# State-space steps of a hybrid encoder block: exponents from running sums read back by row, the z gate from a hyperbolic tangent, and two banks for z

## The reference, cut to what matters

```python
cs = jnp.cumsum((dt * a).reshape(bsz, c, q, g, hg), axis=2)
seg = cs[:, :, :, None] - cs[:, :, None, :]
mask = jnp.tril(jnp.ones((q, q), bool))[None, None, :, :, None, None]
decay = jnp.where(mask, jnp.exp(jnp.where(mask, seg, 0.0)), 0.0)
cb = jnp.einsum('bcqgn,bcsgn->bcqsg', cc, bc)
wts = cb[..., None] * decay
y_diag = jnp.einsum('bcqsgh,bcsghp->bcqghp', wts, xdt)
...
y_off = jnp.einsum('bcqgn,bcghpn->bcqghp', cc, prev) * jnp.exp(cs)[..., None]
```

```python
y = y.reshape(bsz, l, SSD_INNER) * jax.nn.silu(z.astype(F32))
y = y.reshape(bsz, l, SSD_GROUPS, SSD_INNER // SSD_GROUPS)
y = y * lax.rsqrt(jnp.mean(y * y, -1, keepdims=True) + RMS_EPS)
```

## Time and profile before

| | |
|---|---|
| median of 3 runs | 2182.41 us (2177.91 to 2184.29) |
| profiled execution | 2182.37 us, its span 2180.5 us |
| mean granted TensorE clock | 0.952 |
| TensorE busy | 1980.1 us, 91% |
| VectorE busy | 601.0 us, 28% |
| ScalarE busy | 381.4 us, 17% |
| GpSimd busy | 217.7 us, 10% |
| chain that ended last | TensorE 60%, DMA 28%, VectorE 3%, ScalarE 2% |

### The profile page before, as it was taken

How to read it: one execution, slowest core, us unless ns; L and a number is a source line. 1 busy time by engine, 2 the same in 40 slices (tenths; PEclk the granted TensorE clock), 3 DMA queues, 4 the chain that set the end, 5 groups by cost and what they waited for, 6 DMA issues and landing times.

```text
span 2180.5 us, 19987 instructions
## 1 busy us (share of the span) xinstructions
PE 1980.1 (91%) x8382; PEld 938.9 (43%) x8382; DVE 601.0 (28%) x1101; ACT 381.4 (17%) x684; POOL 217.7 (10%) x238
## 2 busy tenths in 40 slices
PE   8989999999989999799988988988988988988887
PEld 4646554456654445434333333334333333333332
DVE  6598756487731115200100100100100100100102
ACT  1334312267740002010000000000000000000001
POOL 1776400022200000000000000000000000000001
PEclk9899999999989999899999999999989999999999
DMA  5622312100104245899999999999999999999995
GB/s 142 126 71 76 112 42 86 58 29 30 58 29 164 69 169 249 356 423 424 428 427 428 428 427 426 428 427 427 428 426 427 428 426 426 429 426 427 428 426 214
DMA packets 88073, 625.47 MB, mean 287 GB/s; under 512 B 21180, under 2 KB 34736, under 8 KB 57776
## 3 DMA queue, kind: packets, MB, share of 16 engines
q1 hardware_dynamic: 75552, 616.41, 68.9%
q10 hardware_dynamic: 12432, 7.79, 1.2%
HBM read 614.39 MB, written 9.78 MB: 286 GB/s over the span
## 4 chain that ended last, share of the span: by engine, by line
PE 60%; DMA 28%; DVE 3%; ACT 2%; issue 1%; POOL 1%; SPq 0%; DVEq 0%; POOLq 0%
PE ps L947 59%; DMA arena<-in_w_e 28%; ACT arena L612 1%; PE ps L1062 0%; DVE arena L1863 0%; DVE arena L1861 0%; DVE arena L1791 0%; DVE arena L1954 0%; DVE arena L1911 0%; ACT L612 0%; POOL arena L492 0%; PE ps L1432 0%; PE ps L1122 0%; DVE arena L1752 0%; DVE arena L1948 0%
## 5 line engine op out<-in xcount | busy, mean ns | idle before, releaser
L947 PE MATMUL ps<-arena 128*64 128x512 f32 (+6 forms) x7850 | 1915.3, 528 | 168.8 <-DMA arena<-in_w_e 107.5
L947 PEld LDWEIGHTS ps<-arena 128*64 128x64 f32 (+2 forms) x7850 | 876.1, 163 | 1183.0 <-issue 1044.5
L612 ACT ACTIVATE arena<-ps 128x512 f32<-128x512 f32 (+5 forms) x292 | 164.8, 595 | 1661.8 <-PE ps L947 954.5
L1920 DVE TENSOR_TENSOR arena<-arena,ps 128x512 f32<-128x512 f32 (+1 forms) x48 | 30.2, 644 | 575.3 <-PE ps L947 575.3
L604 POOL TENSOR_TENSOR arena<-arena 128x1024 f32<-128x1024 f32 x3 | 7.1, 2355 | 1366.2 <-ACT arena L612 1366.2
L1929 DVE TENSOR_TENSOR arena<-arena,ps 128x512 f32<-128x512 f32 x48 | 33.1, 690 | 332.0 <-PE ps L947 332.0
L612 ACT ACTIVATE arena<-arena 128x128 f32<-128x128 f32 (+8 forms) x250 | 110.0, 503 | 82.9 <-DVE arena L1827 20.8
L612 ACT ACT_TABLE_LOAD x74 | 94.9, 1283 | 23.5 <-issue 21.8
L1711 DVE SCALAR_TENSOR_TENSOR arena<-arena 128x512 f32<-128x512 f32 x80 | 60.2, 753 | 2.8
L1911 DVE TENSOR_TENSOR arena<-arena 128x512 f32<-128x512 f32 x8 | 5.6, 694 | 181.9 <-PE ps L1432 181.8
L592 POOL TENSOR_TENSOR arena<-arena 128x768 f32<-128x768 f32 x16 | 24.4, 1524 | 101.2 <-PE ps L947 101.2
(11 more groups left out here) (192 smaller groups left out, 679.8 us busy)
## 6 DMA issues: line engine op xcount, KB each, us to landing
arena<-in_w_e SPq DMA_DIRECT2D x120, 2816.0 KB, 29.3
arena<-in_w_e SPq DMA_DIRECT2D x80, 2048.0 KB, 27.7
arena<-in_w_e SPq DMA_DIRECT2D x16, 1408.0 KB, 22.0
arena<-in_w_in SPq DMA_DIRECT2D x9, 2048.0 KB, 8.4
arena<-in_w_e SPq DMA_DIRECT2D x16, 1024.0 KB, 30.6
arena<-in_w_in SPq DMA_DIRECT2D x5, 1536.0 KB, 6.4
arena<-in_w_out_ssd SPq DMA_DIRECT2D x4, 1536.0 KB, 6.7
gate_scratch<-arena ACTq DMA_DIRECT2D x16, 256.0 KB, 2.4
```

The lines of the kernel that those rows point to most:

```text
L612: return act.activation(out, in_, func, **kw)
L947: return pe.matmul(out, lhsT, rhs, start=a, stop=z)
L1920: tt(o, o, ps[:, i, 0:w], ALU.mult).then_inc(s.hid_ready, 1)
```

## The change

The exponents are no longer products. The running sums of dt·a, which TensorE already forms for another use in bank 5, are copied to `cum` (SBUF, a column per chunk and head), transposed on TensorE, and stored as rows in HBM (`cum_dram`) before the S5 stage. In each step SP loads the rows of six heads and both directions to all 128 partitions (`cum_rows`, two buffers), GpSimd subtracts the token's own sum (`diff_f`, `diff_b`), VectorE takes the smaller of the two directions, and ScalarE takes the exponential in place. Banks 2 and 3 come free: the scores alternate between banks 4 and 2, and z tiles between banks 0 and 3. The four columns of B·C sums of a group are formed at once, and `diag_x` for four chunks at once.

The gate becomes a tanh of z / 2 on ScalarE and a product `(tanh + 1) * z` on VectorE, with the factor 0.5 put into the norm. VectorE's state terms stay in PSUM, and what waited for `y_read` now waits for `gate_ready`.

```diff
+            sp.wait_ge(s.y5_stored, 16 * 2 * T * NQ)
+            sp.wait_ge(s.g_stored, 16 * GATES)
+            sp.wait_ge(s.cum_stored, 16)
+            for i in range(GROUPS * TT):
+                g, c = divmod(i, TT)
+                if i >= 2:
+                    sp.wait_ge(s.diff_ready, i - 1)
+                rows = cum_dram[:, HEADS * c + HG * g:HEADS * c + HG * g + HG, :].rearrange("d h q -> d (h q)")
+                sp.dma_start(cum_rows[:, i % 2].rearrange("p d h q -> p d (h q)"), rows.partition_broadcast(P)).then_inc(cum_loaded[i % 2], 16)
+                if i in (6, 10, 14):
+                    slices(FIRST_Z + 2 + (i - 6) // 4, FIRST_Z + 3 + (i - 6) // 4)
...
+                pool.wait_ge(cum_loaded[i % 2], 16 * (i // 2 + 1))
                 if i >= 1:
-                    pool.wait_ge(s.segm_ps, i)
-                pool.tensor_tensor(rhs_f, first(m_le, HG), last(da[:, c, f], P), ALU.mult)
-                pool.tensor_tensor(rhs_b, first(m_ge, HG), last(da[:, c, b], P), ALU.mult).then_inc(s.mats_ready, 1)
+                    pool.wait_ge(s.diff_min, i)
+                h = slice(HG * g, HG * g + HG)
+                pool.tensor_tensor(diff_f, cum_rows[:, i % 2, 0], last(cum[:, 0, c, h], P), ALU.subtract)
+                pool.tensor_tensor(diff_b, cum_rows[:, i % 2, 1], last(cum[:, 1, c, h], P), ALU.subtract).then_inc(s.diff_ready, 1)
...
-                f(zg[g % 2][:, c, :], ps[:, int(g * TT + c == 1), 0:GI], ACT.Silu).then_inc(s.z_silu, 1)
+                f(zg[g % 2][:, c, :], ps[:, z_bank[c % 2], 0:GI], ACT.Tanh, scale=0.5).then_inc(s.z_tanh, 1)
...
-                act.wait_ge(s.segm_ps, i + 1)
-                if i >= 1:
-                    act.wait_ge(s.g_ready, i)
-                f(emat.rearrange("p (a b) q -> p a (b q)", a=2), ps[:, 2:4, 0:GI], ACT.Exp).then_inc(s.segm_exp, 1)
+                act.wait_ge(s.diff_min, i + 1)
+                f(emat, emat, ACT.Exp).then_inc(s.segm_exp, 1)
...
                 if t >= 2:
-                    pe.wait_ge(s.z_silu, t)
+                    pe.wait_ge(s.z_silu, t - 1)
...
-                pe.wait_ge(s.mats_ready, i + 1)
-                if i >= 1:
-                    pe.wait_ge(s.segm_exp, i)
-                for a in range(2):
-                    o = ps[:, 2 + a, 0:GI].rearrange("p (h q) -> p h q", h=3)
-                    mm(o, m_gt, rhs_f[:, 3 * a:3 * a + 3, :], True, False)
-                    r = mm(o, m_lt, rhs_b[:, 3 * a:3 * a + 3, :], False, True)
-                r.then_inc(s.segm_ps, 1)
...
                 if g + 1 < GROUPS and c < TT - 1:
-                    pe.wait_ge(s.y_read, i + 1)
+                    pe.wait_ge(s.gate_ready, i + 1)
                     added_states(g + 1, c)
...
+            def z_doubled(t):
+
+                g, c = divmod(t, TT)
+                dve.wait_ge(s.z_tanh, t + 1)
+                z = zg[g % 2][:, c]
+                stt(z, z, 1.0, ps[:, z_bank[c % 2], 0:GI], ALU.add, ALU.mult).then_inc(s.z_silu, 1)
+
+            def decay_exponents(i):
+
+                dve.wait_ge(s.diff_ready, i + 1)
+                tt(emat, diff_f, diff_b, ALU.min).then_inc(s.diff_min, 1)
...
+            decay_exponents(0)
             for j in range(TT - 1):
                 weighted_x(0, j)
+                if j == 0:
+                    z_doubled(0)
                 if j == 1:
                     mixing_matrix(0)
+                    decay_exponents(1)
                 carry(0, j)
             mixing_matrix(1)
+            decay_exponents(2)
             for i in range(GROUPS * TT):
...
                 if i >= 1:
                     normalized(i - 1)
+                if i + 1 < GROUPS * TT:
+                    z_doubled(i + 1)
                 if more:
                     weighted_x(g + 1, c)
-                y0, y1, y2 = ty[:, 0], ty[:, 1], ty[:, 2]
-                n.done(tt(h3(y0), h3(xs[:, c, gi]), bc(diag_x[:, i % 2]), ALU.mult))
+                y0, terms = ty[:, 0], []
+                n.done(tt(h3(y0), h3(xs[:, c, gi]), bc(diag_x[:, g % 2, c]), ALU.mult))
                 dve.wait_ge(s.yd_ps, i + 1)
                 if c >= 1:
-                    n.done(tt(h3(y1), h3(ps[:, 6, 0:GI]), bc(e_cs[:, c, f]), ALU.mult))
+                    terms.append(ps[:, 6, 0:GI])
+                    n.done(tt(h3(terms[-1]), h3(terms[-1]), bc(e_cs[:, c, f]), ALU.mult))
...
-                tt(y0, y0, ps[:, 5, 0:GI], ALU.add).then_inc(s.y_read, 1)
-                dve.wait_ge(s.y_read, i + 1)
+                y = ps[:, 5, 0:GI]
+                n.link(tt(y, y, y0, ALU.add))
                 dve.wait_ge(s.z_silu, g * TT + c + 1)
-                tt(ty[:, 3], y0, zg[g % 2][:, c], ALU.mult).then_inc(s.gate_ready, 1)
+                tt(ty[:, 3], y, zg[g % 2][:, c], ALU.mult).then_inc(s.gate_ready, 1)
                 if i + 2 < GROUPS * TT:
                     mixing_matrix(i + 2)
+                if i + 3 < GROUPS * TT:
+                    decay_exponents(i + 3)
                 if more:
                     carry(g + 1, c)
```

More of the change, by code:

```diff
@@ L200, in encoder @@
         dt_bias, a_neg = C.take(2 * HEADS), C.take(2 * HEADS)
-        dt_step, diag_x = C.take(TT, HEADS), C.take(2, HG)
+        dt_step, diag_x = C.take(TT, HEADS), C.take(2, TT, HG)
         d_row, norm_g, ln1_cols = C.take(HEADS), C.take(INNER // P), C.take(2, KT)
@@ L277, in encoder @@
         S = Space(arena, S2.at - 4 * SEQ, top)
-        rhs_f, rhs_b = S.take(HG, P), S.take(HG, P)
+        diff_f, diff_b = S.take(HG, P), S.take(HG, P)
         bc_prod = S.take(SEQ)
+        cum_rows = S.take(2, 2, HG, P)
+        score_bank = (4, 2)
+        z_bank = (0, 3)
         S = Space(arena, late_at, top)
@@ L340, in encoder @@
         slice_loaded = [sem(f"slice_loaded_{i}") for i in range(NW)]
+        cum_loaded = [sem(f"cum_loaded_{i}") for i in range(2)]
         unit_loaded = [sem(f"unit_loaded_{i}") for i in range(LANDINGS)]
@@ L1035, in _ @@
             mm(ps[:, 6, 0:8 * H].rearrange("p (c h) -> p c h", c=TT), ones, da, True, True).then_inc(s.seg_ps, 1)
+            pe.wait_ge(s.seg_exp, 1)
+            for d in range(2):
+                r = pe.transpose(ps[0:TT * H, 3, P * d:P * d + P], cum[:, d].rearrange("p c h -> p (c h)"), ident)
+            r.then_inc(s.seg_ps, 1)
             def toeplitz(q):
@@ L1053, in states @@
                 pe.wait_ge(s.u_loaded, 16 * 2 * T)
+                if q == 0:
+                    pe.wait_ge(s.seg_exp, 2)
                 if q >= 1:
@@ L1141, in added_states, with scores @@
                     mm(ps[:, 6 + d, 0:GI], bn[:, c, P * g:P * g + P], xw[:, d, :], True, True).then_inc(s.st_ps, 1)
-            def scores_and_segments(i):
+            def scores(i):
                 g, c = divmod(i, TT)
-                q = slice(P * c, P * c + P)
-                if i >= 1:
[L1147 to L1150, removed]
-                pe.wait_ge(s.mats_ready, i + 1)
-                if i >= 1:
-                    pe.wait_ge(s.segm_exp, i)
-                for a in range(2):
-                    o = ps[:, 2 + a, 0:GI].rearrange("p (h q) -> p h q", h=3)
-                    mm(o, m_gt, rhs_f[:, 3 * a:3 * a + 3, :], True, False)
-                    r = mm(o, m_lt, rhs_b[:, 3 * a:3 * a + 3, :], False, True)
-                r.then_inc(s.segm_ps, 1)
+                if i >= 2:
+                    pe.wait_ge(s.g_ready, i - 1)
+                if c == 0:
+                    pe.wait_ge(s.bc_ready, g + 1)
+                    for k in range(TT):
+                        mm(ps[:, score_bank[0], P + k:P + k + 1], bc_prod[:, P * k:P * k + P], ones[:, 0:1], True, True)
+                q = slice(P * c, P * c + P)
+                mm(ps[:, score_bank[i % 2], 0:P], bT[:, g, q], cT[:, g, q], True, True).then_inc(s.cb_ps, 1)
             def y_products(i):
@@ L1166, in y_products @@
                 if i >= 1:
-                    pe.wait_ge(s.y_read, i)
+                    pe.wait_ge(s.gate_ready, i)
                 if c >= 1:
@@ L1192, in _ @@
             pe.wait_ge(s.nat_copied, 16)
-            scores_and_segments(0)
+            scores(0)
             pe.wait_ge(s.silu_done, 20)
@@ L1198, in _ @@
                     z_tile(0, j + 1, w)
-            pe.wait_ge(s.z_silu, 2)
-            scores_and_segments(1)
+            scores(1)
             for i in range(GROUPS * TT):
@@ L1204, in _ @@
                 if i + 2 < GROUPS * TT:
-                    scores_and_segments(i + 2)
+                    scores(i + 2)
                 if i >= 1:
@@ L1226, in _ @@
                     pe.wait_ge(s.yt_copied, 3 * GROUPS * TT)
-                    pe.wait_ge(s.y_read, GROUPS * TT)
+                    pe.wait_ge(s.gate_ready, GROUPS * TT)
                 for half in range(halves):
@@ L1742, in carry @@
                         dve.tensor_copy(to, ps[:, 6 + d, 0:GI]).then_inc(s.carried, 1)
-            def mixing_matrix(i):
+            def z_doubled(t):
[6 more added lines that the diff above has]
```

(14 more changed lines are left out.)

34 lines of the change are left out of this document (21 added, 13 removed).

## The result

The changed kernel takes 2200.68 us (median; 2199.17 to 2202.29) against 2182.39 before, a ratio of 1.0087 with a 95% interval of 1.0069 to 1.0105. The forecast was 2199.

What follows compares the result with a forecast made beforehand. The prediction took TensorE to bound the kernel, busy 91% of the span. Loop -2.3, clock +14.4 and start +4.8 us made +16.9 on 2182.4, so 2199 us, with a range of 2181 to 2213.

Steps and rivals of the forecast that it cites:

- TensorE was the bound, and the products taken off it had filled its wait for VectorE: In the steps TensorE sets the pace, busy 47.69 of 48.00 us a group; segment products, 43 us, filled its wait.
- The loop at 47.6 us a group: Between gate products in the steps: 12.8, 12.8, 11.0 and 11.0 us, 47.6 a group; all intervals together -2.3 us.
- The last group at 11.0 a step: In the last group of steps, two steps set by ScalarE at 11.0 us each, the last as it was, 6.0.
- the arm with matrices: ScalarE's work in a step, from the gate product through the root and six matrices to the tanh: 6.4 us.
- The clock, 14.4 us: TensorE's waits in the steps lower its clock: long wait 2.8 us, two short 1.0 each, 14.4 over three groups.
- The start, 4.8 us: Before the first gate product, VectorE's minimum on loaded rows precedes weighted_x: 4.8 us later, bounds 2 and 8.
- Costs at nothing: In the S5 stage, column products, transposes, copies and store cost nothing during TensorE's 6.00 us wait; uncovered, about 1 us.
- rival D: In the steps the row loads are late, each step about 1 us longer: about 2212 us; chance 0.11.
- Rival B: In the steps the clock holds through TensorE's waits and the loop is right: 2182 to 2185 us; chance 0.22.
- Rival C: In the steps VectorE's own work sets the pace, 38.6 us a group, not the loop: 2158 us; chance 0.12.
- The sum: Whole kernel: -2.3 + 14.4 + 4.8 = +16.9 us on 2182.4, giving 2199.

Runs made afterwards that it cites:

- the idle products: Changed kernel with 6 (c = 0) or 3 (c = 1, 2) extra TensorE products before the wait for the gate product; 2184.68 us, ratio 1.0016.
- the rows early: Changed kernel with the first two row loads issued ahead of the two z slices instead of behind them; 2198.29 us, ratio 1.0075.
- the run with the tanh first: Changed kernel with ScalarE's tanh of step i + 2 issued ahead of the six matrices of step i + 3; 2198.78 us, ratio 1.0086.
- the edit with z first: Changed kernel with TensorE's z tile of step i + 2 ahead of the gate product's wait and the added states; 2181.27 us, ratio 1.0002.
- the two reordered engines: Changed kernel with TensorE's z tile ahead of the gate product's wait and ScalarE's tanh ahead of the six matrices; 2170.21 us, ratio 0.9955.
- the long wait filled: Changed kernel with 6 extra TensorE products before the gate product's wait at c = 0 alone; 2194.03 us, ratio 1.0065.

## Why the prediction was right, point by point

- **TensorE was the bound, and the products taken off it had filled its wait for VectorE.** Right. The products went, and TensorE waits for L1839 ten times, 33.5 us. Nine of these are the forecast ones; at c = 2 they are 2.0 us and not 3.0, since the next group's four column sums, formed at once, take 1.0 us of TensorE there, work that I had counted at nothing.
- **The loop at 47.6 us a group.** Right, shown where the clock was kept: 12.8 + 12.8 + 11.1 + 10.7 = 47.4. That the z tile stands in it is shown by moving it: 23 us less from first to last gate product.
- **The last group at 11.0 a step.** Too long by 2.5 us in one of them: the interval 13 to 14 is 8.5, because step 13 has no matrices left to build and the tanh comes 2.3 us sooner. I had counted the arm with matrices.
- **The clock, 14.4 us.** Right that it falls and decides the sign, too small in size. Against the intervals with the clock kept (12.8, 12.8, 11.1) the nine of the changed kernel are 18.9 us longer, about 2.1 for each of the three kinds of wait, where I had 2.8 for the long and 1.0 for the short ones. My reason for the 1.0, that some falls may not come, failed: all nine came. Of the 18.9 the idle products gave back 16; the other 2.9 are the first interval's, which they don't reach.
- **The start, 4.8 us.** The sign and size were near (5.8 to 6.5 measured), the reason half right. That the chain begins only when the rows have landed holds: with the rows early the start is 4.1 us shorter. That they delay it through weighted_x does not: moving that gave nothing. What costs is VectorE's dense chain of minimum, mixing matrices and sums behind the rows, and in it 3.4 us behind GpSimd, a stall that I had left to the range and counted only for the loop.
- **Costs at nothing.** The transposes and copies in the S5 stage: the second z slice is issued at 422.0 to 427.5 from one trace to the next and was at 424.4 before, so a cost there is not seen, and one of 1 us could not be. The row loads land in 5.0 us (median of sixteen), and GpSimd's differences wait for VectorE's minimum twelve times and in the loop for no load, so rival D had no ground. The stalls of VectorE beside GpSimd in the loop are there and end before the tanh comes, as forecast, but from c 3 to 0 only just: the run with the tanh first shows a second arm of the same length there.
- **Rival B** would have been the result with the clock kept: 2184.7 measured, 2182 to 2185 forecast. **Rival C** needed y products that don't stand behind the z tile. That is the edit with z first, and only together with the tanh does it bring VectorE near its own bound (43.4 a group with the stalls in it; I had reckoned 38.6).
- **The sum.** 2199 for 2200.7, +16.9 for +17.3 between the traced executions. So close a hit is partly luck: the clock was 4.5 us too low and the start up to 1.7, while the loop without the clock was 2.6 too high, and the parts ahead and behind, which I had at nothing, happened to be 3.1 us shorter in this execution. The mechanism, the sign and the group of 47.6 us are not luck.

What stays open: whether the silu and the early rows gain anything on top of the two reordered engines, and why the clock falls behind one wait of 2 us and not behind another of 3.7. Not run is the new order with the products left in. TensorE was busy for 47.69 of a group's 48.00 us then, so the order alone could hardly have shortened a group; that is an argument and not a measurement.

## What to carry to other kernels

Before taking work off the busiest engine, ask what that engine would wait for if the work were gone: here it filled the other engine's part of a circle, and 43 us of products were worth nothing until the order around them changed. Walk the circle once per kind of step with durations from the trace; it came within 0.2 us for a full group. And treat a wait of 2 us that returns in every step as dearer than it looks, since the products behind it may run at half clock for a few us: fill it with the next step's independent work.

## What the runs showed of the hardware

A repeated wait of TensorE of 2.0 to 2.9 us was followed by the 1.2 GHz level in all six cases of the changed kernel, as one of 4.9 was, and in five of six with the long wait filled; waits of 1.0 us between idle products and added states were not. A longer wait is no sure sign: with z first one of 3.7 us passed at 1.00. Adding 36 idle products made the changed kernel 16 us faster. A TENSOR_SCALAR with its one operand in SBUF, 0.42 us alone, took up to 1.73 beside GpSimd's 768-column operations: it is held back like the operations with two SBUF operands, while those with an operand in PSUM were not (z_doubled took its 0.56 us at 563.69 in the run with the tanh first, with GpSimd's L610 running).
